# Attention sections: softmax maps woven between projection and output products, turned in blocks, differential maps combined before the value products

## The reference

```
for layer in range(DEPTH):
    proj = rmsnorm(x, ln1_g[layer]) @ w_in[layer]
    qa, ka, va, cq, ckv, kr, qc, kc, vc = jnp.split(proj, split_idx, axis=-1)
    out_a = mixer_dilated(qa, ka, va, cos64, sin64)        # 6 heads of 64
    out_b = mixer_mla(cq, ckv, kr, ...)                    # 6 heads, q and k 96 wide, v 64
    out_c = mixer_diff(qc, kc, vc, ...)                    # 4 heads, 2 maps each, q and k 32 wide
    x = x + concatenate([out_a, out_b, out_c]) @ w_o[layer]
```

## Time and profile before

| what | value |
|---|---|
| median of 3 runs | 2090.44 us (2090.26 to 2091.22) |
| profiled execution, its own time | 2091.79 us |
| its span, first to last instruction | 2089.7 us |
| busy: TensorE, its weight loads | 2004.5 us (96%), 1689.2 us (81%) |
| busy: VectorE, ScalarE, GpSimd | 1276.3 us (61%), 973.2 us (47%), 95.7 us (5%) |
| chain of work that ended last | TensorE 88%, VectorE 5%, ScalarE 5% |
| mean granted TensorE clock | 0.971 of full |

### The profile page before, as it was taken

One profiled execution on the slowest core, in us unless ns is written; L12 is line 12 of the kernel. 1 busy time (PEld: TensorE's weight loads), 2 busy tenths in 40 slices (PEclk: granted clock), 3 DMA queues, 4 the chain that ended last, 5 costly groups with the idle time before them and its releaser, 6 DMA issues.

```text
span 2089.7 us, 26278 instructions
## 1 busy us (share of the span) xinstructions
PE 2004.5 (96%) x10800; PEld 1689.2 (81%) x10800; DVE 1276.3 (61%) x1587; ACT 973.2 (47%) x1233; POOL 95.7 (5%) x124
## 2 busy tenths in 40 slices
PE   6999999999999999999998899999999999999998
PEld 5778888877888787788887688889888888778887
DVE  4755655665665665577665466666665667447564
ACT  5544443653544544454445454445354454345443
POOL 0400000030000000001100000000000000000000
PEclk9889999979999999999999999999999999999999
DMA  7503665521655564356553346655465655445561
GB/s 243 178 1 124 199 187 176 178 81 41 200 194 185 181 204 160 121 171 201 185 178 112 112 142 191 198 165 172 161 212 184 199 192 191 146 132 178 187 198 61
DMA packets 197151, 340.62 MB, mean 163 GB/s; under 512 B 6758, under 2 KB 128234, under 8 KB 197033
## 3 DMA queue, kind: packets, MB, share of 16 engines
q1 hardware_dynamic: 193024, 331.04, 48.6%
q10 hardware_dynamic: 4008, 7.90, 1.1%
HBM read 337.88 MB, written 1.05 MB: 162 GB/s over the span
## 4 chain that ended last, share of the span: by engine, by line
PE 88%; DVE 5%; ACT 5%; issue 1%; DMA 0%; POOL 0%; DVEq 0%; ACTq 0%
PE ps L484 19%; PE ps L486 18%; PE ps L485 18%; PE ps L592 13%; PE ps L590 8%; PE ps L589 2%; ACT w_hi L928 2%; PE ps L845 1%; DVE w_lo L1386 1%; PE ps L739 1%; PE ps L754 1%; ACT xT L968 1%; PE ps L747 1%; PE ps L746 1%; ACT arena L962 1%
## 5 line engine op out<-in xcount | busy, mean ns | idle before, releaser
L1386 DVE TENSOR_TENSOR w_lo<-w_raw,w_hi 128x2048 fp32r<-128x2048 f32 x316 | 728.7, 2312 | 283.1 <-ACT w_hi L928 282.6
L928 ACT ACTIVATE w_hi<-w_raw 128x2048 fp32r<-128x2048 f32 x316 | 600.6, 1912 | 127.8 <-PE ps L486 121.5
L484 PE MATMUL ps<-w_hi,u_h 128*128 128x512 f32 (+1 forms) x1056 | 419.2, 397 | 9.3 <-DVE u_l L1803 2.9
L592 PE MATMUL ps<-xT,w_hi 128*128 128x512 f32 x1176 | 419.2, 396 | 0.0
L485 PE MATMUL ps<-w_lo,u_h 128*128 128x512 f32 (+1 forms) x1056 | 413.7, 392 | 0.0
L486 PE MATMUL ps<-w_hi,u_l 128*128 128x512 f32 (+1 forms) x1056 | 413.6, 392 | 0.0
L590 PE MATMUL ps<-xT,w_lo 128*128 128x256 f32 x1344 | 347.3, 279 | 0.0
L484 PE MATMUL ps<-w_hi,xT 128*128 128x512 f32 (+2 forms) x800 | 289.1, 361 | 7.6 <-DVE w_lo L1386 5.1
L485 PE MATMUL ps<-w_lo,xT 128*128 128x512 f32 (+2 forms) x800 | 285.1, 356 | 0.0
L486 PE MATMUL ps<-w_hi,xT 128*128 128x512 f32 (+2 forms) x800 | 284.8, 356 | 0.0
L590 PEld LDWEIGHTS ps<-xT,w_lo 128*128 128x128 f32 x1344 | 253.4, 189 | 13.6
(11 more groups left out here) (202 smaller groups left out, 1852.7 us busy)
## 6 DMA issues: line engine op xcount, KB each, us to landing
w_raw<-mlp_w_dram SPq DMA_DIRECT2D x128, 1024.0 KB, 5.5
w_raw<-ret_w_in_dram SPq DMA_DIRECT2D x48, 1024.0 KB, 5.2
w_raw<-w_up_dram SPq DMA_DIRECT2D x32, 1024.0 KB, 5.6
w_raw<-w_down_dram SPq DMA_DIRECT2D x32, 1024.0 KB, 4.9
w_raw<-w_in_dram SPq DMA_DIRECT2D x16, 1024.0 KB, 7.1
w_raw<-ret_w_out_dram SPq DMA_DIRECT2D x16, 1024.0 KB, 4.9
w_raw<-cf_w_pw_dram SPq DMA_DIRECT2D x12, 1024.0 KB, 5.4
w_raw<-sc_w_in_dram SPq DMA_DIRECT2D x12, 1024.0 KB, 5.2
```

The source lines that it names most:

```text
L484: pe.matmul(dst, lh, rh, start=start, stop=False)
L592: ins = pe.matmul(ps[:, bank, :], w_hi[:, slot, wsl], both, start=False, stop=kc == KC - 1)
L928: act.activation(w_hi[:, slot, :], w_raw[:, slot, :], ACT.Copy).then_inc(hi_ready[slot], 1)
L1386: tt(w_lo[:, slot, :], w_raw[:, slot, :], w_hi[:, slot, :].bitcast(F32), ALU.subtract).then_inc(lo_ready[slot], 1)
```

## The change

- **Order of tiles.** Groups 2, 3 and 4 come first, then `w_uq` (tile 6) and `w_ukv` (7), then group 0 (8, 9), group 1 (10, 11), and the output tiles in reverse order (12 to 15).
- **Loop of 25 stages** (`STAGES`), with differential maps first, then latent, then dilated. Stage 16 starts no map. At the end of each stage `filler` puts a quarter of a weight tile: `w_ukv` and group 0 in stages 0 to 7, group 1 in 8 to 15, output tiles 12 and 13 in 16 to 23. Tiles are prepared in halves within the stages.
- **Blocks.** Four differential maps, or two dilated heads, are turned with four transposes of full width; the score products then read 32 or 64 rows of the block.
- **Normalising.** VectorE scales the probabilities in SBUF before they are turned. For the second map of a differential head it adds its scaled map to the first, so a differential head is turned and multiplied once.
- **Values.** For latent and dilated heads the values are stationary and the turned probabilities move. Two heads fill the upper and lower 64 partitions of one PSUM bank, and the result comes out already transposed as an output operand. Only the differential heads are turned (`turn_c`).
- **PSUM.** One bank each for turned blocks, scores, turned probabilities and values. ScalarE copies odd sets of turned probabilities, VectorE even ones.
- **Rotations.** VectorE rotates the differential queries and keys before the loop and 256 columns of dilated keys at stage 16; GpSimd rotates the latent queries and 512 columns of dilated ones, and then takes the root of the head norm.

```diff
-GROUPS = (2, 3, 0, 1, 4)
-UQ, UKV, LAST_A, LAST_B = 8, 10, 9, 11
+GROUPS = (2, 3, 4, 0, 1)
+UQ, UKV, MID_TILE, LATE_TILE, OUT_TILE = 6, 7, 8, 10, 12
...
+BLOCKS = 2 + BH + AH // 2
+SETS = CH + BH + AH
+STAGES, LATE = MAPS + 5, 16
+FED = {CH: 1, CH + 1: 3, CH + 2: 4, CH + 3: 5, CH + 4: 6, CH + 5: 7}
+C_FED, B23_B45_FED, B01_FED, A01_FED, A45_FED, A23_FED = 2, 3, 4, 5, 6, 7
...
+        def map_at(s):
+            return s if 0 <= s < LATE else s - 1 if LATE < s <= MAPS else None
...
+                def turn_block(m):
+                    b = block_of(m)
+                    q, k, d = block_cols(b)
+                    if b == 0:
+                        pe.wait_ge(rope_c.sem, rope_c.at(sec, 1))
+                    if b == 2:
+                        pe.wait_ge(rope_b.sem, rope_b.at(sec, 1))
+                        pe.wait_ge(kv_half.sem, kv_half.at(sec, 2))
+                    if b == 2 + BH:
+                        pe.wait_ge(rope_a.sem, rope_a.at(sec, 1))
+                    if b == 3 + BH:
+                        pe.wait_ge(rope_a_late.sem, rope_a_late.at(sec, 1))
...
+                        pe.wait_ge(feed_lo.sem, feed_lo.at(sec, C_FED))
+                    pe.wait_ge(qkT_sb.sem, qkT_sb.at(sec, b))
+                    for j, v in enumerate((q, k)):
+                        for t in range(NT):
+                            ins = pe.transpose(ps[0:d, 4, j * S + t * P:j * S + (t + 1) * P], v[:, t, :], ident[:])
...
+                def scores(m):
+                    b, r = block_of(m), rows_of(m)
+                    pe.wait_ge(qkT_sb.sem, qkT_sb.at(sec, b + 1))
+                    pe.wait_ge(max_ready.sem, max_ready.at(sec, m))
+                    pe.matmul(ps[:, 5, 0:P], qkT[r, b % 2, 0:P], qkT[r, b % 2, S:S + P], start=True, stop=True)
+                    pe.matmul(ps[:, 5, P:P + S], qkT[r, b % 2, P:S], qkT[r, b % 2, S:2 * S], start=True,
+                              stop=True).then_inc(scores_ready.sem, 1)
...
+                def turn_probs(m):
+                    e = set_of(m)
+                    pe.wait_ge(norm_done.sem, norm_done.at(sec, m + 1))
+                    if e > 0:
+                        pT_copied(e - 1)
+                    for j in range(3):
+                        ins = pe.transpose(ps[:, 6, j * P:(j + 1) * P], sm[:, slot_of(m), j * P:(j + 1) * P], ident[:])
+                    ins.then_inc(pT_ready.sem, 1)
...
+                def values_pair(e):
+                    i = pv_of(e)
+                    pT_copied(e - 1)
+                    pT_copied(e)
+                    if i == CH:
+                        pe.wait_ge(pv_sb.sem, pv_sb.at(sec, CH))
+                    else:
+                        pe.wait_ge(feed_lo.sem, feed_lo.at(sec, FED[i - 1]))
+                    for k in range(2):
+                        for o in range(2):
+                            v = value_of(e - 1 + o)
+                            cols = slice(k * P, S)
+                            ins = pe.matmul(ps[64 * o:64 * o + 64, 7, cols], v[:, k, :], pT[:, (e - 1 + o) % 3, 2 * k * P:2 * P + k * P],
+                                            start=k == 0, stop=k == 1)
+                    ins.then_inc(pv_ready.sem, 1)
...
+                def filler(s):
+                    if s == 0:
+                        latent_values()
+                    if s < 8:
+                        if s == 0:
+                            pe.wait_ge(kv_half.sem, kv_half.at(sec, 1))
+                        wide_chunk(MID_TILE + s // 4, s // 4, 2, s % 4)
+                    elif s < 16:
+                        if s == 8:
+                            pe.wait_ge(kv_half.sem, kv_half.at(sec, 2))
+                        wide_chunk(LATE_TILE + (s - 8) // 4, (s - 8) // 4, 0, s % 4)
+                    elif s < 24:
+                        pe.wait_ge(feed_lo.sem, feed_lo.at(sec, C_FED if s < 20 else B23_B45_FED))
+                        out_chunk((s - 16) // 4, s % 4)
+                for s in range(STAGES):
+                    m = map_at(s)
+                    turn = m is not None and first_of_block(m)
+                    if turn and s != LATE + 1:
+                        turn_block(m)
+                    if s == LATE - 1:
+                        turn_c()
+                    m = map_at(s - 1)
+                    if m is not None:
+                        scores(m)
+                    m = map_at(s - 3)
+                    if ends_set(m):
+                        turn_probs(m)
+                    m = map_at(s - 4)
+                    if ends_set(m):
+                        e = set_of(m)
+                        if e < CH:
+                            values_c(e)
+                        elif e % 2:
+                            values_pair(e)
+                    if turn and s == LATE + 1:
+                        turn_block(map_at(s))
+                    filler(s)
...
+                pe.wait_ge(feed_lo.sem, feed_lo.at(sec, A45_FED))
+                for h in range(2):
+                    late_out(0, 0, 0, h)
+                    late_out(0, 1, 0, h)
+                    late_out(1, 0, 0, h)
+                pe.wait_ge(feed_lo.sem, feed_lo.at(sec, A23_FED))
+                for h in range(2):
+                    late_out(1, 1, 0, h, True).then_inc(acc_ready.sem, 1)
+                for h in range(2):
...
+                for s in range(STAGES):
+                    m = map_at(s)
+                    turn = m is not None and first_of_block(m)
+                    if turn and s != LATE + 1:
+                        block_out(m)
+                    if s == LATE - 1:
+                        act.wait_ge(feed_T.sem, feed_T.at(sec, 1))
+                        act.activation(u_h[:, 0, :, :].rearrange("p a b -> p (a b)"), ps[:, 4, :], ACT.Copy).then_inc(feed_hi.sem, 1)
+                    m = map_at(s - 3)
+                    if ends_set(m) and set_of(m) % 2:
+                        e = set_of(m)
+                        act.wait_ge(pT_ready.sem, pT_ready.at(sec, e + 1))
+                        if e >= 3:
+                            act.wait_ge(pv_ready.sem, pv_ready.at(sec, pv_of(e - 3) + 1))
+                        act.activation(pT[:, e % 3, :], ps[:, 6, 0:384], ACT.Copy).then_inc(pT_a.sem, 1)
+                    m = map_at(s - 1)
+                    if m is not None:
                         act.wait_ge(max_ready.sem, max_ready.at(sec, m + 1))
                         for t in range(NT):
                             c = slice(0, P) if t == 0 else slice(P, P + S)
...
+                            j = 2 * (m % 4) + t
+                            ins = act.activation(sm[:, m % 4, c], sm[:, m % 4, c], ACT.Exp, bias=negmax[:, j:j + 1], scale=-1.0,
                                                  accum_out=zsum[:, j:j + 1])
                         ins.then_inc(probs_ready.sem, 1)
...
+                    m = map_at(s - 4)
+                    if m is not None and m >= C_MAPS and m % 2:
+                        i = pv_of(set_of(m))
+                        act.wait_ge(pv_ready.sem, pv_ready.at(sec, i + 1))
+                        if i == CH + 5:
+                            act.wait_ge(used[sec.slot(OUT_TILE)], sec.fill(OUT_TILE) + 1)
+                        act.activation(pair_out(i)[0], ps[:, 7, 0:S], ACT.Copy).then_inc(feed_hi.sem, 1)
+                    if turn and s == LATE + 1:
+                        block_out(map_at(s))
+                    if s <= 3:
+                        prepare_half(sec, 7 + s // 2, s % 2)
+                    elif s % 4 in (1, 2):
+                        prepare_half(sec, 8 + s // 4, s % 4 - 1)
+                    if s == 8:
+                        evac(sec, 3)
+                    if s == LATE - 1:
+                        evac(sec, 4)
+                prepare(sec, 14)
...
+                for t in range(NT):
+                    ins = rotate(pool, step, pr[:, t, 0:512].rearrange("p (h d) -> p h d", d=AD), 512 // AD, AD // 2,
+                                 rope[:, t, 0:32], rope[:, t, 32:64], rope_pa, rope_pb)
...
+                def normalise(m):
+                    j, second = 2 * (m % 4), m < C_MAPS and m % 2 == 1
+                    vec.wait_ge(probs_ready.sem, probs_ready.at(sec, m + 1))
+                    step.link(vec.reciprocal(rz[:, j:j + 2], zsum[:, j:j + 2]))
+                    if second:
+                        step.link(ts(rz[:, j:j + 2], rz[:, j:j + 2], neglam[:, sec.layer:sec.layer + 1], None, ALU.mult))
+                        vec.wait_ge(norm_done.sem, norm_done.at(sec, m))
+                    for t in range(NT):
+                        c = slice(0, P) if t == 0 else slice(P, P + S)
+                        if second:
+                            first = sm[:, slot_of(m), c]
+                            ins = stt(first, sm[:, m % 4, c], rz[:, j + t:j + t + 1], first, ALU.mult, ALU.add)
                         else:
...
+                            ins = ts(sm[:, m % 4, c], sm[:, m % 4, c], rz[:, j + t:j + t + 1], None, ALU.mult)
```

(58 more changed lines are left out.)

509 lines of the change are left out of this document (261 added, 248 removed).

## The result

The changed kernel takes 2041.59 us (median of 4 runs, 2040.44 to 2043.44), the kernel before 2090.35 (4 runs, 2088.38 to 2091.22): ratio 0.9771, 95% interval 0.9757 to 0.9786. It is 48.8 us faster. The forecast was 2039, 2.6 us under the median.

A forecast was written before the change was run, and what follows sets the result against it. TensorE, busy 96% of the span, was taken as the bound, so only its work, idle time and half clock could pay. Savings of 25.7 and 25.3 us, together 51.0, took 2091.79 to 2040.8, forecast as 2039 (2024 to 2060).

The forecast's parts named there:

- idle time removed: TensorE's waits around the map loops of both attention sections all go: 7.3 us in the first, 6.7 in the second.
- half clock removed: Clock stays full through the map loops and their drains: 17.5 us saved in the first section, 17.7 in the second.
- TensorE's work, with shape changes: Fewer transposes and paired values save 10.4 us a section; added changes of product shape cost 3.5 (1 to 6).
- new waits: TensorE's added waits in the new loop, mostly for VectorE and GpSimd: 6 us a section (3 to 14).
- rival A: Clock still falls for 10 to 13 us per section, costing 5 to 6.5 each: about 2051 us; chance 0.14.
- The maxima of the first stages: TensorE's next scores wait for VectorE's maxima, with one scores bank, in the loop's first maps: about 1.7 us.
- Stage 17: The late rotation of 256 columns on VectorE, about 2.3 us, stands ahead of a block: 1 us of wait.
- a root that comes late: VectorE and TensorE wait for the head norm's root, queued behind GpSimd's rotation of some 8 us: 1.5 us.
- signs that I gave for being right: Full clock in both loops, no TensorE wait over 1 us, stages 3.0 to 3.3 us, scores awaiting maxima only early.
- B: VectorE or GpSimd sets the loop's pace; TensorE waits 6 to 10 us more per section: about 2055 us; chance 0.12.
- C: Hand-offs do not overlap, stages last 4.5 us, 34 us more per section: 2107 us, slower than before; chance 0.05.
- D: Combined and paired steps cost what they save, clock stays low, only idle time is gained: 2076 us; chance 0.03.

The follow-up runs named there:

- e5: Kernel before with ten extra full products ahead of the map loop and 2, 3 and 10 more in its first three stages: 2070.94 us, 0.9908.
- e2: Changed kernel with its weight chunks and their tile splitting moved out of the loop, ahead of it or behind it: 2089.29 us, 1.0006 to the kernel before.
- e4: Changed kernel with VectorE's two halves of tile 14 moved from stages 15 and 16 to 17 and 18: 2034.31 us, 0.974 to the kernel before.
- e3: Changed kernel with GpSimd's rotation of the dilated maps cut from eight heads to one, computation partly left out: 2034.99 us, 0.9743 to the kernel before.
- e6: Changed kernel with GpSimd's 512-column rotation cut into four pieces of 128 columns: 2042.18 us, 0.9775 to the kernel before.
- e1: Kernel before with ten extra full products, results unused, in TensorE's idle time ahead of the map loop: 2089.5 us, 1.0001.
- e8: Changed kernel with moved tile halves, earlier last-group copy, late rotation in two parts and GpSimd's rotation in 128-column pieces: 2028.59 us, 0.9704 to the kernel before.
- e7: Changed kernel with moved tile halves, VectorE's last projection-group copy earlier and its late rotation in two parts: 2033.29 us, 0.9725 to the kernel before.
- e10: Changed kernel with a pair's four value products issued head by head instead of alternating column halves: 2041.71 us, 0.9768 to the kernel before.

## Why the prediction was right, point by point

For both sections together, what was predicted and what the trace of the changed kernel shows:

| term | predicted | measured |
|---|---|---|
| idle time removed | 14.0 | 14.0 |
| half clock removed | 35.2 | 31.4 |
| TensorE's work, with shape changes | 13.8 | 19.5 (remainder) |
| new waits | −12 | −15.1 |
| sum | 51.0 | 49.8 |

The sum is nearer than its terms: 3.8 us less from the clock and 3.1 us more of waits were made up by 5.7 us more from TensorE's work, and that is luck.

*Idle time and its filling.* Right. None of the waits of the earlier trace rows is left, and the new ones were booked apart.

*Half clock.* The mechanism was right in the main: e5 fills the idle time of the kernel before and the clock stays, e2 takes the weaving out of the changed kernel and the clock goes. Whether the filled time or the heavy products in it did it, no run separates. The size was 3.8 us too large: 3.4 and 6.8 us at half are left, in which TensorE works some 3.6 and 4.1 (the stretches from 122.40 and 433.00), half of it lost. A small piece of rival A came true, at the place of the longest new wait. My check by six maps at 4.43 against 2.04 gave 14.3 with the wrong partner: by e5's 2.37 it is 12.4, about as far from the 13 us on the other side.

*TensorE's work.* Better than said, by 2.9 us a section. This is what the sum of 49.8 leaves when the other rows are taken off, not a row of its own. 1.2 of it is measured: six pairs at 0.80 in place of 1.0. The other 1.7 I cannot place. I looked at the change of shape, in a stage of the changed kernel with nothing but scores and a chunk (TensorE in order of time):

```profile
65.34 0.48 PE L808 MATMUL ps<-arena 32*128 32x128 f32 x2
65.67 0.59 PE L809 MATMUL ps<-arena 32*128 32x256 f32 x2
66.19 0.50 PE L550 MATMUL ps<-w_hi,xT 128*128 128x512 f32 x1
66.53 0.40 PE L551 MATMUL ps<-w_lo,xT 128*128 128x512 f32 x1
```

The first weight product behind the scores takes 0.34 to the next start, the following ones 0.23. So a change costs the 0.1 us that I took, and the number of changes (35 a section) was at the high side if anything was.

*Waits.* 15.1 in place of 12, inside 6 to 28, but with the wrong list, which nearly cancelled:

- The maxima of the first stages: 1.7 predicted, none found. VectorE's 25.50 us in 27.40 were near the bound and did not cross it. The step that failed set VectorE's work against TensorE's stage by stage, at the upper end of my prices for it; the whole stretch has 1.9 us to spare.
- Copies of the latent values: 0.6 predicted, 0.74.
- Stage 17: 1.0 predicted, 4.2 (1.34 + 2.86). This is the mis-sized term. I priced the eight instructions of the late rotation and forgot that two half tiles, a pair's copy and the normalising stand ahead of it in the same queue. e4 shows it: moving the half tiles alone takes 2.3 us of it and the clock's fall with it.
- GpSimd: 1.5 predicted, for a root that comes late. 2.2 measured, but with no late root: the rotation lasted the 8 us I gave it, and what it cost was VectorE's normalising beside it (e3). The late root comes only with e6's pieces.
- The last pair: 0.5 predicted, none found.

Two of the signs that I gave for being right did not come: there are three TensorE waits over 1 us a section, and the scores wait for maxima in stages 9 and 10, not in the first ones.

*Rivals.* A came true for some 4 us of 10 to 13. B's price (6 to 10 us more a section) was paid to 1.5. C did not occur: from the first chunk at 63.74 to the end of the last pair at 143.0 the 25 stages took 79.3 us, 6.8 of waits among them, 3.2 each, against my 3.15 and the 4.2 from which C decides. Even e2, which leaves the hand-offs bare, took under 3 us a stage. D is refuted by the changed kernel's own time and clock. e2 shows the part of it that holds: without the weaving the clock stays low and the leaner maps give nothing.

## What to carry to other kernels

Where an engine's clock falls behind a short wait and then stays low through a stretch of small work, price the wait by the stretch behind it: here 7 us of idle time a section cost another 17. Fill it with independent work in small pieces all along, not with one block ahead, for the block only moves the wait (e1). Then look at the single stage where the most is queued on the engine beside it; moving two half tiles by two stages was worth 6.5 to 7.3 us, more than either of the finer edits behind it.

## What was not expected of the hardware

- A short VectorE instruction can be the one that loses beside GpSimd: 0.81 to 2.67 us and 0.55 to 2.21 us for two instructions of 128 and 256 columns, beside GpSimd products of 1.3 us, and 1.03 and 0.76 beside pieces of 0.5 us (e3, e6). The cost follows the length of GpSimd's instruction.
- Maps of 64 rows, with their transposes, keep a full clock when nothing idles ahead of them (e5, three maps from 93.1 on), though in the kernel before the same maps ran for over 16 us at half without regaining it.
- The clock fell for 3.4 us behind waits of 0.69 and 0.65 us in one section of e8, and held behind the same waits in the other section and behind 1.23 us in e7. How much of a run is at half differs between executions of one kernel as well (a mean granted clock of 0.990 and 0.988 in e7).
- Two column halves take 0.80 us together in either order of issue (e10).
